# Reordering the last three groups of projections and the convolution taps of pair 6

## The reference, cut to what matters

```python
u = rms_norm(h, norm_mix[l])
proj = u @ w_in[l]                        # 512 x 2048 @ 2048 x 5408
conv_val = proj[..., :D_CONV]             # "val", 8 tiles of 128 channels
conv_gate = proj[..., D_CONV:2 * D_CONV]  # "gate", 8 tiles
# conformer_conv: u = val * sigmoid(gate); 31 taps per channel; layer norm; silu
# rwkv7_time_mix: proj + (prev_frame(proj) - proj) * mu, split in r, k, v and low-rank parts
def step(S, inp):                         # scan over 512 tokens, per head 64 x 64
    rt, wt, kt, vt, at, bt = inp
    sa = jnp.einsum('bhvk,bhk->bhv', S, at)
    S = S * wt[:, :, None, :] + sa[..., None] * bt[:, :, None, :] + vt[..., None] * kt[:, :, None, :]
    return S, jnp.einsum('bhvk,bhk->bhv', S, rt)
mixed = jnp.concatenate([y_conv, y_rwkv], axis=-1)
h = h + mixed @ w_out[l]
```

## Time and profile before

| | us |
|---|---|
| median of three runs | 3819.63 |
| lowest and highest run | 3815.98 and 3819.87 |
| the profiled execution's own time | 3817.81 |
| its span | 3816.1 |
| TensorE busy in the span | 3477.0 |
| VectorE busy | 1468.0 |
| ScalarE busy | 568.6 |
| GpSimd busy | 487.6 |

### The profile page before, as it was taken

One profiled execution on the slowest core, in us unless ns is written; L12 is line 12 of the kernel. 1 busy time (PEld: TensorE's weight loads), 2 busy tenths in 40 slices (PEclk: granted clock), 3 DMA queues, 4 the chain that ended last, 5 costly groups with the idle time before them and its releaser, 6 DMA issues. The chain is left out here.

```text
span 3816.1 us, 51345 instructions
## 1 busy us (share of the span) xinstructions
PE 3477.0 (91%) x21663; PEld 2366.1 (62%) x21663; DVE 1468.0 (38%) x2520; ACT 568.6 (15%) x1088; POOL 487.6 (13%) x440
## 2 busy tenths in 40 slices
PE   8999999997899887777777759999999999999999
PEld 5877777775545432322232218754588888888888
DVE  4567677787312200000000014573133354454442
ACT  2223222222202100000000003101100010331000
POOL 1410100100000000000000000032000000465511
PEclk9999999998999899999999989999999999999999
DMA  3312121113051799999999986335333322223432
GB/s 110 83 51 63 41 64 50 53 51 125 23 191 56 312 421 422 422 422 422 420 421 417 419 323 165 95 76 124 106 107 106 111 81 88 78 89 103 155 109 76
DMA packets 321260, 672.81 MB, mean 176 GB/s; under 512 B 43228, under 2 KB 227974, under 8 KB 267685
## 3 DMA queue, kind: packets, MB, share of 16 engines
q1 hardware_dynamic: 312293, 639.50, 46.2%
q0 software_dynamic: 8768, 30.42, 2.2%
HBM read 639.58 MB, written 47.05 MB: 180 GB/s over the span
## 5 line engine op out<-in xcount | busy, mean ns | idle before, releaser
L2658 PE MATMUL stream_bank<-whole_big 128*128 128x256 f32 x3584 | 783.2, 380 | 1.0 <-DVE whole_big L3779 0.6
L2658 PEld LDWEIGHTS stream_bank<-whole_big 128*128 128x128 f32 x3584 | 678.8, 190 | 98.0 <-issue 4.5
L2132 PE MATMUL experts_run_bank<-whole_big 128*64 128x512 f32 x2048 | 486.1, 621 | 174.5 <-DMA whole_big<-in_expert_w_gate 102.4
L310 PE MATMUL first_bank<-whole_big 128*128 128x256 f32 x2240 | 537.5, 389 | 0.0
L2132 PEld LDWEIGHTS experts_run_bank<-whole_big 128*64 128x64 f32 x2048 | 169.3, 142 | 490.7 <-issue 490.4
L310 PEld LDWEIGHTS first_bank<-whole_big 128*128 128x128 f32 x2240 | 413.9, 191 | 90.3 <-issue 30.1
L2709 DVE TENSOR_TENSOR whole_big<-stream_bank,whole_big 128x256 f32<-128x256 f32 x292 | 119.4, 422 | 429.1 <-PE stream_bank L2658 429.0
L2563 PE MATMUL stream_bank<-whole_big 128*128 128x512 f32 x640 | 278.8, 594 | 0.0
L2152 PE MATMUL experts_run_bank<-whole_big 128*64 128x512 f32 x1024 | 230.0, 596 | 35.5 <-DMA whole_big<-in_expert_w_down 23.2
L2197 DVE TENSOR_TENSOR whole_big<-whole_big,experts_run_bank 128x512 f32<-128x512 f32 x16 | 11.0, 687 | 650.5 <-PE experts_run_bank L2132 650.5
L2563 PEld LDWEIGHTS stream_bank<-whole_big 128*128 128x128 f32 x640 | 120.2, 190 | 145.5 <-issue 145.1
(11 more groups left out here) (480 smaller groups left out, 3682.1 us busy)
## 6 DMA issues: line engine op xcount, KB each, us to landing
whole_big<-in_expert_w_gate SPq DMA_DIRECT2D x128, 1024.0 KB, 27.2
whole_big<-in_expert_w_up SPq DMA_DIRECT2D x128, 1024.0 KB, 29.5
whole_big<-in_expert_w_down SPq DMA_DIRECT2D x128, 1024.0 KB, 26.5
whole_big<-in_w_in SPq DMA_DIRECT2D x110, 1024.0 KB, 5.9
whole_big<-in_w_out SPq DMA_DIRECT2D x16, 1024.0 KB, 7.5
whole_big<-in_w_out SPq DMA_DIRECT2D x8, 2048.0 KB, 12.9
gates_two<-whole_big SPq DMA_DIRECT2D x40, 256.0 KB, 7.6
whole_big<-gates_two POOLq DMA_DIRECT2D x40, 256.0 KB, 3.0
```

Source lines behind the costliest of these rows:

```text
L310: mm = pe.matmul(self.place(m), weights[:, k, :], left[:, k, :], start=(k == 0), stop=(k == 7))
L2132: mm = pe.matmul(bank[self.half(h), :], self.x_T[:, PARTS * q + k, self.half(h)], self.ring[slot][:, k, :], start=(q == 0 and k == 0), sto ...
L2658: mm = pe.matmul(self.place[m % 3], weights[:, k, :], left[:, k, :], start=(k == 0), stop=(k == self.k - 1))
```

## The change

Four things change.

1. `UNITS_ONE`: the last two groups change places. Group 18 becomes val and gate of tile 7, group 19 r and k of pair 7 (before it was the other way round). The order of the weight loads follows the list.
2. `FULL_SHARE` has 4 units instead of 3 in slot A1, in each of pairs 0 to 5. `LAST_SHARE` has 30 units instead of 36: slot L2 has 2 instead of 4, L2b none instead of 4.
3. `CONV_LAST`: the 48 taps of pair 6 stand in other slots. Slots A2 to L3b have 23 instead of 13, M 6 instead of 4, S1 to S6 none instead of 8, Y none instead of 4.
4. `key_scale(j + 1)` on VectorE stands behind the work of slot L2b instead of ahead of it.

```diff
+UNITS_ONE = UNITS_ONE[:-4] + UNITS_ONE[-2:] + UNITS_ONE[-4:-2]
...
-FULL_SHARE = (4,) + (3,) * 15 + (2,) * 6 + (3,)
-LAST_SHARE = (4,) * 9 + (0,) * 14
+FULL_SHARE = (4, 4) + (3,) * 14 + (2,) * 6 + (3,)
+LAST_SHARE = (4,) * 7 + (2,) + (0,) * 15
...
-CONV_LAST = (0, 3, 0, 2, 2, 2, 2, 3, 2, 0, 0, 2, 2, 6, 4, 6, 1, 1, 1, 1, 2, 2, 4)
+CONV_LAST = (0, 3, 1, 3, 3, 3, 3, 3, 3, 2, 2, 2, 2, 6, 6, 6, 0, 0, 0, 0, 0, 0, 0)
...
+                    rest("L2b")
                     if more:
                         key_scale(j + 1)
-                    rest("L2b")
                     level_ev(j, 3)
```

## The result

| | before | after |
|---|---|---|
| median of the runs, us | 3818.3 (16 runs, 3815.38 to 3820.35) | 3826.51 (16 runs, 3823.31 to 3830.57) |
| ratio, with its 95% interval | 1 | 1.0021 (1.0014 to 1.0028) |
| the profiled execution's span, us | 3816.1 | 3824.6 |

The change costs 8.2 us. 3829 had been predicted, and slower with 0.55. Against the 16 runs of before it is 0.21% slower, and the interval leaves 1 out: a small loss, but a real one.

What follows compares the result with a forecast made beforehand. TensorE, busy for 91% of the span, was taken as the bound, losing time only where it waits. Terms summed to +10.7 on 3817.8 us, 3828.5, given as 3829; the forecast's own range was 3826 to 3834, the wider one 3813 to 3837.

Steps and rivals of the forecast that it cites:

- Units: Pairs 0 to 5: six added units at 0.95 us each where TensorE is the bound, +5.7 us.
- Clock behind the waits: Pairs 1 and 4: fills run slowly at the lower clock behind the longer waits, +1.6 us in each.
- Step (a): Pair 6, level 0: the sums leave A2 for A1 and the wait of 2.10 us goes.
- Step (c): Pair 6, level 4: ScalarE's table load and sigmoid move to A1, addition at 903.3 instead of 907.25.
- Step (e): Pair 6, second state step to line 968: without eight taps between, 5.7 us instead of 8.96, 3.3 gained.
- (b): Pair 6, level 3: VectorE's addition comes at about 895.3 instead of 896.47, and TensorE waits 3 to 4 us.
- (d): Pair 6, level 4 to first state step: VectorE never rests, step at 920.2 instead of 922.78, 2.6 us earlier.
- `key_scale`: Placed behind the work of L2b: 0; if ScalarE's cover were gone, 0.6 in each of seven pairs, +4 us.
- Shift as a whole: Pair 7 and all behind it start from the end of pair 6 and only shift, without a term of their own.
- The added waits mostly do not come: Pairs 1, 3 and 4: VectorE's slack halves their 14.2 us, pair 6 still gains; 3821 us, chance 0.33.
- The end of pair 6 is worth more: Level 4 to pair 6's end: shorter waits keep the clock up, up to 6 us more; 3808 to 3810, chance 0.12.
- The clock follows the waits: Pairs 1, 3 and 4: clock stays down behind waits over 3 us, 3 us more in each; 3838, chance 0.10.

Runs made afterwards that it cites:

- spread sums and its old share: Kernel before the change, own shares, order and taps, with the three sums given out one by one to slots where VectorE rests; 3801.2 us.
- the best kernel: Kernel before the change with sums given out one by one, one unit more in each of pairs 2 to 5, 32 instead of 36 in pair 6; 3793.3 us.
- shares alone: Kernel before the change with only FULL_SHARE and LAST_SHARE of the changed kernel; 3824.3 us, ratio 1.0018.
- after, old taps: Changed kernel with CONV_LAST of before, everything else as changed; 3824.1 us, ratio 1.0019.
- six units in pair 5: Changed kernel, but pairs 0 to 4 keep the shares of before and pair 5 takes all six added units; 3818.6 us, ratio 1.0002.
- `key_scale` alone: Kernel before the change with only key_scale moved behind the work of slot L2b; 3817.3 us, ratio 1.0000.
- the units early in pair 6: Changed kernel, but pairs 0 to 5 keep the shares of before and pair 6 takes its 36 units in its first seven slots; 3822.2 us.

## Why the prediction was right

The mechanism held: TensorE waits where the sums and the takes with shifts meet a late VectorE, and the shares moved them there. That the time came so close is in part luck. Of the 10.7 us forecast, pairs 0 to 6 brought 8.3; pair 7 added 3.6 and the opening took 2.5 off, neither of them foreseen, and 0.9 less stood behind pair 7.

**Bound and places: right.** Nearly all waits came where and as long as worked out: 5.75 for 5.7 in L1b of pair 1 (2.3 + 3.4), 4.69 for 4.8 in its steps, 1.44, 0.59 and 1.46 for 1.4, 0.6 and 1.5 in pair 3, 3.60 for 3.6 in pair 4, 1.97 for 2.0 in its steps, 1.20 for 0.59 + 0.7 in pair 0, 3.40 for 3 to 4 at level 3 of pair 6. The 2.14 of pair 2 is gone. In pair 5 0.38 remained of the first (none was expected) and 0.90 of the second (1.3 expected). The 3.6 of pair 4 counted on GpSimd's gating beside the sums, and it was there: one sum took 2.17 us beside a gating of 2.18.

```profile
673.38 2.17 DVE L331 TENSOR_TENSOR whole_big<-whole_big 128x1024 f32<-128x1024 f32 x1
```

**Units: 5.2 for 5.7.** Pair 3 went from 102.15 with spread sums and its old share to 103.01 in the best kernel with one unit more, both without a wait: 0.86 each, six of them 5.2.

**Clock behind the waits: not shown.** 1.6 was put down in pair 1 and in pair 4. One profile each gives 0.4 and 1.6: in pair 1 the waits grew by 3.4 + 0.7 and the unit is 0.9, of 5.4 in all; in pair 4 the waits grew by 3.1 (3.60 + 0.10 - 0.61) and the unit is 0.9, of 5.6. But the profiles of other kernels with the same waits in these pairs differ by as much. With the waits of before, pair 1 took 111.8 to 113.2 in four profiles and pair 4 106.1 to 107.7; with those of after, pair 1 took 117.8 to 118.6 in three and pair 4 112.0 to 113.3. So the clock's share lies between -0.4 and 1.8 in pair 1 and between 0.3 and 3.3 in pair 4, and the term stays open. Pair 1 stayed 1.3 us below its forecast and pair 4 0.6, most of the 2.4 by which pairs 0 to 6 stayed below the sum.

**Pair 6: the right path, put down to the wrong edits.** -5.9 was predicted and -5.9 measured, and each station came within 0.7 us of its forecast. Counted from the pair's start:

| start of | before | forecast | after | shares alone | after, old taps |
|---|---|---|---|---|---|
| level 3's addition | 57.7 | 56.6 | 56.3 | 53.5 | 55.4 |
| level 4's addition | 68.5 | 64.6 | 63.9 | 61.4 | 62.6 |
| the copy before the first step | 84.0 | 81.5 | 81.2 | 76.9 | 78.1 |
| the next pair | 102.6 | 96.7 | 96.7 | 95.4 | 96.7 |

What failed is which edit brings it. The shares alone give -7.2, the order +1.2, the taps 0.0. Step (a) is right, the 2.10 at level 0 is gone; a wait at level 2 that it did not have came instead, 1.28, and 0.55 with the old taps or the shares alone:

```profile
896.88 1.15 PE L781 MATMUL first_bank<-whole_big 64*64 64x64 f32 x32 [1.28 <-DVE whole_big L1204]
```

Step (c) put the table load's move down to the order, but the load leaves this place with the shares alone, and the wait for ScalarE at level 4 falls from 3.64 to 2.12. The order takes it on to 0.81, but the shifts of r and k that changed places with the sigmoid cost more: the order loses 1.2 us, and 2.6 in the best kernel. Step (e) is right in itself, 3.1 for 3.3, but its price stands elsewhere: the eight taps of the steps and the four of Y now stand on the way to the first step, which comes 3.1 later than with the old taps. The prediction had them inside (b) and (d) and never set them against (e), so it credits the taps with 3.3 where their balance is nothing. And (b) and (d) hid how much the shares bring: 7.2, more than the whole.

The Trainium skill ("ScalarE: Activation LUTs", What ACT_TABLE_LOAD costs) would have given step (c) up to 1.4 more by its drain. Pair 6 came out at the sum without it, and after the change too the sigmoid starts right behind its load (859.64 + 1.28, then 860.94); no run here shows that drain.

**`key_scale`: right.** 0, ratio 1.0000 (0.9991 to 1.0009).

**Pair 7 and the opening: not foreseen.** "Shift as a whole" failed: +3.6 and -2.5 (last section). By the two medians the change costs 8.2, by the spans 8.5. How much of the 8.2 is pair 7 can't be told from one profile.

**The rivals.** "The added waits mostly do not come" fell: pairs 0 to 5 grew by 14.2. "The end of pair 6 is worth more": its granted clock stayed at 0.86, and the waits ahead of pair 6 stood at far over 3. "The clock follows the waits" fell too: 0.94, 1.00 and 0.97 in pairs 1, 3 and 4, and none of the three grew by more than its forecast. Taken as this rival takes it, the rule of the Trainium skill ("TensorE: Matmul & The Clock Gate", What's actually happening) that the throttled state is the default went too far: pair 3 kept a granted clock of 1.00 with waits of 1.44, 0.59 and 1.46.

## What to carry to other kernels

Where one engine fills gaps by a schedule of shares, a unit's own price (0.9 us) is small beside what it shifts on the other engines: read, for each slot, what comes ahead of the instruction that the bounding engine waits for. Long helper work with a late deadline should be split and put by slack rather than by a fixed lag: the same 2520 VectorE instructions in another row gave 17 to 25 us, two to three times what the change had lost. A unit moved into a stretch where TensorE is the bound costs its full price, and where another engine was the bound a wait of 3.94 on TensorE cost nothing: find out for each stretch which it is. And if work is moved out of one stretch, add it to the stretch that it enters, in the same line of the sum.

## What the runs showed of the hardware that was not expected

**The same wait is followed by no loss of clock, or by one of 4.7 us.** Before and in the kernel with six units in pair 5, pair 2 has the same instructions and the same wait. Before:

```profile
449.60 1.15 PE L780 MATMUL first_bank<-whole_big 64*64 64x64 f32 x32 [2.14 <-DVE whole_big L1203]
...
454.68 1.99 PE L310 MATMUL first_bank<-whole_big 128*128 128x256 f32 x8
```

With six units in pair 5:

```profile
449.25 1.15 PE L782 MATMUL first_bank<-whole_big 64*64 64x64 f32 x32 [2.15 <-DVE whole_big L1205]
...
457.27 3.78 PE L312 MATMUL first_bank<-whole_big 128*128 128x256 f32 x8
```

A fill of 1.99 takes 3.78, at 1.2 for 2.4 GHz, and the pair 109.1 for 104.4. With `key_scale` alone it was 105.9, with the units early in pair 6 again 104.4. Six units in pair 5 shows it in its profiled execution, the slowest of its eleven. What decides between them was not found: the wait, its place and the instructions before it are the same, the start in the pair differs by nothing, the start in the execution by 0.4 us. Pair 4 does the same with its waits of 1.20 and 2.58: 107.7 at 0.98 in before, 106.1 at 1.00 with six units in pair 5.

**Pair 7 has two lengths.** Its waits are the same in all runs (0.79, 6.27 and 2.58, to 0.05), its length is 114.1 to 115.0 in eight profiles and 117.0 to 118.0 in six. Behind the 2.58 the eight matmuls at line 411 (412 after) take 5.25 for 3.70. The long form came with the new order and taps together (four profiles), but also with the best kernel, which has neither, and not with the units early in pair 6, which has both. So it isn't the taps as such. What goes with it in all fourteen profiles is the clock at the pair's start: pair 6 ends at 1.2 of 2.4 GHz, and this level reaches 8.3 to 9.5 us into pair 7 in the eight short ones and 10.2 to 11.4 us in the six long ones. After the change, for example:

```profile
947.20:958.10 10.90, 10.90 (x80) 6.39 (x79) 4.87 (x5) 0.60 (x1) 2.94 (x2) 0.50 0.01 2
```

What sets where it ends is not shown.

**The opening** reached pair 0 at 200.2 to 200.5 us in five profiles and at 202.7 to 203.1 in the other nine, of kernels that are alike up to there: a difference of 2.5 us between executions, as much as several of the terms above. It is the clock: TensorE's waits up to there are the same (18.7 to 19.0 in all), and the granted clock was at its lower level for 6.8 us in the five and for 10.2 us in the nine. The same 809 matmul instructions keep TensorE busy for 181.6 us after the change and for 184.1 before. A term of this size is read from the pair that it belongs to, not from the total.
